# A hybrid encoder step on one core: the whole last prompt tile goes by fetched expert rows, the bias line is stored in eight pieces, and each v tile brings its own gelu tile

## What is computed

```python
q = (xb @ wq).reshape(nb, PEER_HEADS, 2, PEER_DKEY // 2)           # 8 heads, 2 x 64
s = jnp.einsum('nhpd,hpkd->nhpk', q, sub_keys)                     # 128 keys each
sv, si = lax.top_k(s, PEER_TOPK)                                   # 16 best of either half
cand = (sv[:, :, 0, :, None] + sv[:, :, 1, None, :])               # 256 sums
fv, fi = lax.top_k(cand, PEER_TOPK)                                # 16 experts per head
g = jax.nn.softmax(fv, axis=-1)
u, vv = expert_u[eidx], expert_v[eidx]                             # tables of 16384 x 1024
act = jax.nn.gelu(jnp.einsum('nhkd,nd->nhk', u, xb), approximate=False)
out = jnp.einsum('nhk,nhkd->nd', g * act, vv)
```

## Time and profile before

| | |
|---|---|
| median of 3 runs | 2180.13 us (2179.73 to 2186.38) |
| profiled execution, its own time | 2187.16 us |
| its span, first to last instruction | 2185.4 us |
| busy share of the span: PE, DVE, ACT, POOL | 92%, 59%, 42%, 36% |
| mean granted TensorE clock | 0.961 |
| moved by DMA | 421.70 MB |

### The profile page before, as it was taken

The page is one execution under the profiler, slowest core; times in us unless marked ns, Lnnn a source line. Parts: engine busy times, 40 slices in busy tenths (PEclk is TensorE's granted clock), DMA queues, the critical chain, the costliest instruction groups (busy, mean ns, idle before and its releaser), DMA issues. The chain is left out here.

```text
span 2185.4 us, 32122 instructions
## 1 busy us (share of the span) xinstructions
PE 2011.7 (92%) x11629; PEld 1826.0 (84%) x11629; DVE 1282.9 (59%) x2482; ACT 918.6 (42%) x2008; POOL 797.6 (36%) x780
## 2 busy tenths in 40 slices
PE   7299987998996999999999999996999999999997
PEld 6298876886895998898999999996989889998896
DVE  2014352334613299999999855552566666666666
ACT  4012112224314233585888888882333323323333
POOL 4142322322321201485898888880011111111110
PEclk9699988999997999999999999998999999999999
DMA  6431135222606166788889899988679879889873
GB/s 150 71 87 39 39 127 91 81 77 89 210 20 137 41 178 184 203 256 239 254 233 264 247 265 265 259 255 271 221 253 293 284 252 298 284 273 298 269 252 108
DMA packets 304465, 421.70 MB, mean 193 GB/s; under 512 B 32116, under 2 KB 248692, under 8 KB 300724
## 3 DMA queue, kind: packets, MB, share of 16 engines
q1 hardware_dynamic: 276660, 318.98, 50.4%
q0 software_dynamic: 27648, 100.68, 15.0%
HBM read 346.43 MB, written 72.42 MB: 192 GB/s over the span
## 5 line engine op out<-in xcount | busy, mean ns | idle before, releaser
L1311 PE MATMUL ps<-x_high,uT_high 128*128 128x448 f32 x1024 | 383.9, 375 | 15.8 <-DVE uT_low L1303 15.8
L1888 PE MATMUL ps<-hid_high,v_high 128*128 128x448 f32 x1024 | 376.9, 368 | 22.8 <-DVE hid_low L1861 22.8
L1555 POOL TENSOR_SCALAR area<-iota_row,chosen 128x128 f32<-128x128 f32 x448 | 376.5, 854 | 2.6
L1888 PE MATMUL ps<-hid_low,v_high 128*128 128x448 f32 x1024 | 375.7, 367 | 0.0
L1888 PE MATMUL ps<-hid_high,v_low 128*128 128x448 f32 x1024 | 375.7, 367 | 0.0
L1311 PE MATMUL ps<-x_high,uT_low 128*128 128x448 f32 x1024 | 375.3, 367 | 0.0
L1311 PE MATMUL ps<-x_low,uT_high 128*128 128x448 f32 x1024 | 374.9, 366 | 0.0
L1834 ACT CAST v_high<-area 128x1024 fp32r<-128x1024 f32 x128 | 134.2, 1048 | 448.2 <-PE ps L1888 369.7
L1229 POOL DMA_INDIRECT gathered_rows<-in_peer_v_dram,gathered_index x96 | 96.8, 1009 | 570.1 <-DVE gathered_acc L1261 481.5
L1859 DVE TENSOR_TENSOR v_low<-area,v_high 128x1024 fp32r<-128x1024 f32 x128 | 156.8, 1225 | 233.7 <-ACT v_high L1834 233.7
L1303 DVE TENSOR_TENSOR uT_low<-u_turned,uT_high 128x1024 fp32r<-128x1024 f32 x128 | 159.3, 1244 | 158.8 <-ACT uT_high L1298 158.8
(11 more groups left out here) (289 smaller groups left out, 3731.5 us busy)
## 6 DMA issues: line engine op xcount, KB each, us to landing
u_nat<-in_peer_u_dram SPq DMA_DIRECT2D x512, 128.0 KB, 4.7
area<-in_peer_v_dram SPq DMA_DIRECT2D x128, 512.0 KB, 5.3
hidden<-gelu_out SPq DMA_DIRECT2D x128, 224.0 KB, 3.3
routing<-dense SPq DMA_DIRECT2D x28, 1024.0 KB, 6.1
w_raw<-in_w_in_dram SPq DMA_DIRECT2D x44, 512.0 KB, 4.0
area<-hidden SPq DMA_DIRECT2D x8, 1792.0 KB, 8.6
gelu_in<-hidden SPq DMA_DIRECT2D x8, 1792.0 KB, 9.5
routing_in<-routing SPq DMA_DIRECT2D x8, 1792.0 KB, 16.7
```

The lines of the kernel that those rows point to most:

```text
L1311: ins = self.nc.tensor.matmul(self.k.ps[:, b, 0:N], w[:, b, kk, :], x[:, kk, 0:N], start=(kk == 0 and p == 0), stop=(kk == KD - 1 and p == 2))
L1555: ins = nc.gpsimd.tensor_scalar(first[:, b % AREAS, f, :], iota[:, :], chosen[:, 0, c:c + 1], None, ALU.is_equal)
L1888: ins = nc.tensor.matmul(ps[:, kk, 0:N], v[:, b, kk * P:(kk + 1) * P], h[:, b, :], start=(n == 0 and p == 0), stop=(n == P - 1 and p == 2))
```

## The change

Three edits.

1. `MORE` is now a list of (first frame, frames) of tile 3 that are fetched: [(0, 128)]. All 128 frames of tile 3 fetch their 128 picks each, so `HALVED` = 0, N = 384, the routing has 96 batches and 24 groups of 16 frames in place of 112 and 28, `ALL` = 160 and the matmuls are 128 x 384. The copies that repack picks and x for the two half-tiles of frames fall away but for one each of index and weight. `posf` and `picked` move into an area that is free then. `Plan` is unchanged but reads the new numbers: 160 dots stand in the 110 steps 15 to 124 where 96 stood, and the first batch of routing is at step 46, not 27.
2. `rel_line` is stored in `PIECES` = 8 parts of 384 KB, one behind each of the weight tiles 5 to 12.
3. In `experts` the gelu tile of step n comes right behind v tile n, alone (192 KB), into the slot that step n-8 has left, and the routing tiles of 8 steps come in 4 parts of 384 KB behind four v tiles. The adds are spread evenly over steps 7 to 120.

The core of the diff:

```diff
-FETCHED = P // 2
-SETS = P // FETCHED
-HALVED = P - FETCHED
+MORE = [(0, P)]
+HALVED = min(lo for lo, _ in MORE)
 N = 3 * P + HALVED
...
+PIECES = 8
 AHEAD_LOADS = 64 if HALVED else 48
-MORE = PH * TOPK // SETS
-ALL = PICKS + MORE
+SETS = [P // f for _, f in MORE]
+TAKEN = [PH * TOPK // n for n in SETS]
+FROM = [PICKS + sum(TAKEN[:j]) for j in range(len(MORE) + 1)]
+ALL = FROM[-1]
+COPIES = 2 * sum(SETS)
...
             for i in range(2, EARLY + 4):
                 load_tile(i)
-                if i == 5:
+                if 5 <= i < 5 + PIECES:
                     sp.wait_ge(line_done, 1)
-                    sp.dma_start(k.line_dram, bcast(line, 1, P)).then_inc(line_stored, 16)
+                    rows = slice((i - 5) * P // PIECES, (i - 4) * P // PIECES)
+                    sp.dma_start(k.line_dram[:, rows], bcast(line, 1, P // PIECES)).then_inc(line_stored, 16)
...
         if m % ALL >= PICKS:
-            pool.wait_ge(self.more_ready, 32 * SETS)
+            pool.wait_ge(self.more_ready, 16 * COPIES)
         after(pool, self.used, m - RING + 1)
...
         @block.sync
         def _(sp):
-            def load_oct(q):
+            def load_routing(q, i):
+                groups = slice(NGRP * i // PARTS, NGRP * (i + 1) // PARTS)
                 after(sp, hid_low_done, OCT * (q - 1))
-                sp.dma_start(gelu[q % 2], k.gelu_dram[q * OCT:(q + 1) * OCT].rearrange("a j n -> j a n")).then_inc(in_loaded[q % 2], 16)
-                sp.dma_start(routing[q % 2].rearrange("j g a n -> j g (a n)"),
-                             k.route_dram[:, :, q * OCT:(q + 1) * OCT, :].rearrange("g j a n -> j g (a n)")).then_inc(in_loaded[q % 2], 16)
-
-            load_oct(1)
+                sp.dma_start(routing[q % 2][:, groups].rearrange("j g a n -> j g (a n)"),
+                             k.route_dram[groups, :, q * OCT:(q + 1) * OCT, :].rearrange("g j a n -> j g (a n)")).then_inc(in_loaded[q % 2], 16)
+
             for n in range(V, P):
                 sp.wait_ge(v_low_done, n - V + 1)
                 sp.dma_start(v_nat[:, n % V, :], peer_v[0, n * P:(n + 1) * P, :]).then_inc(v_loaded[n % V], 16)
-                if n % OCT == 2 and n // OCT + 1 < P // OCT:
-                    load_oct(n // OCT + 1)
+                if n >= OCT:
+                    sp.wait_ge(hid_low_done, n - OCT + 1)
+                    sp.dma_start(gelu[:, n % OCT, :], k.gelu_dram[n]).then_inc(v_loaded[n % V], 16)
+                q, i = divmod(n + OCT - V, OCT)
+                if i < PARTS and q < P // OCT:
+                    load_routing(q, i)
...
-                if n >= 8 and n % 5 != 0 and (n - 8) * 4 // 5 < ALL:
+                while added[0] < min(ALL, (n - 6) * ALL / (P - 14)):
                     gathered.add(dve, added[0])
                     added[0] += 1
```

More of the change, by code:

```diff
@@ L1231, in fetch, with part @@
                                           ).then_inc(self.fetched[m % RING], 16)
+    @staticmethod
+    def part(m):
+        return sum(m >= f for f in FROM[:-1])
     def arrived(self, eng, m):
@@ L1367, in _ @@
                 sp.dma_start(gathered.x[g * TS:(g + 1) * TS, 0, :], gathered.x[0:TS, 0, :]).then_inc(gathered.x_ready, 16)
[L1368 to L1371, removed]
+            sp.wait_ge(row_scaled, 1 + len(MORE))
+            copies = EXTRA - 1
+            for j, (lo, frames) in enumerate(MORE):
+                for g in range(SETS[j]):
+                    if g * frames != lo:
+                        copies += 1
+                        sp.dma_start(gathered.x[g * frames:(g + 1) * frames, 1 + j, :], gathered.x[lo:lo + frames, 1 + j, :]).then_inc(gathered.x_ready, 16)
+            sp.wait_ge(gathered.x_ready, 16 * copies)
         @block.scalar
@@ L1515, in step @@
                     sp.wait_ge(pick_done, 1)
[L1516 to L1519, removed]
+                    for j, (lo, frames) in enumerate(MORE):
+                        rows, mine = slice(lo, lo + frames), slice(FROM[j], FROM[j + 1])
+                        for g in range(SETS[j]):
+                            to, picks = slice(g * frames, (g + 1) * frames), slice(g * TAKEN[j], (g + 1) * TAKEN[j])
+                            sp.dma_start(gathered.index[to, mine], flat[rows, picks]).then_inc(gathered.more_ready, 16)
+                            sp.dma_start(gathered.weight[to, mine], picked[rows, 2, picks]).then_inc(gathered.more_ready, 16)
                 for b in plan.routing.get(n - 3, []):
@@ L1797, in experts @@
     V = 4
+    PARTS = 4
     v_nat, v_loaded, in_loaded, gelu, routing = k.v_nat, k.v_loaded, k.in_loaded, k.gelu_in, k.routing_in
-    gelu = (gelu[0], hold("gelu_in1", [P, OCT, N])[:, :, :])
+    gelu = gelu[0]
     routing = (routing[0], hold("routing_in1", [P, NGRP, OCT, GRP])[:, :, :, :])
@@ L1920, in _ @@
                 if t == 3:
-                    for c in range(2):
-                        ins = nc.tensor.matmul(ps[HALVED:P, 2 * t + c, :], same[:, TS:], gathered.acc[:, 1, c * 512:(c + 1) * 512], start=True, stop=True)
+                    for j, (lo, frames) in enumerate(MORE):
+                        cols = slice(TS + lo - HALVED, TS + lo - HALVED + frames)
+                        for c in range(2):
+                            ins = nc.tensor.matmul(ps[lo:lo + frames, 2 * t + c, :], same[:, cols], gathered.acc[:, 1 + j, c * 512:(c + 1) * 512],
+                                                   start=True, stop=True)
                 ins.then_inc(turned, 1)
```

50 lines of the change are left out of this document (29 added, 21 removed).

## The result

| | before | after |
|---|---|---|
| median of 7 runs each, us | 2179.73 (2173.55 to 2186.38) | 2158.23 (2147.05 to 2169.22) |
| ratio after / before | | 0.9898, interval 0.9868 to 0.9929 |
| span of the profiled execution, us | 2185.4 | 2155.2 |
| mean granted TensorE clock | 0.961 | 0.947 |

The account below looks back on a forecast made before the run. PE was taken as busiest, with DVE, POOL and DMA just under it. Terms -30 - 3 + 40 + 22 - 67 = -38 us took the profiled 2187.2 to 2149, or 2142 us at the median; range 2085 to 2210.

Parts of the forecast that it names:

- What bounds the kernel: Whole kernel: PE has the largest share; the change moves its work to DVE, POOL and DMA, which stand just under it.
- Narrower matmuls: `search` and `experts`: 384 columns take 0.174 and 0.177 us a matmul, 175 us less PE work in all.
- `rel_line` in pieces: Projection: weight tiles no longer wait behind the whole store, so PE's stall shrinks; -30 us, bounds -41 and -15.
- Steps 0 to 14: Start of `search`, 749 to 830 us: a narrower matmul gives back at most DVE's time without a dot; -3 us.
- With the sort: `search`, 830 to 1232 us: DVE, 98% busy with 97 dots for 58, sets the length; +40 us, bounds +26 and +53.
- third rival: `search` from step 46: POOL is locked for all of DVE's two-input time; sum +52, 2232 us; chance 0.08.
- After the sort: `search`, 1232 to 1482 us: POOL, stretched by DVE's two-input work, needs 272 us; +22 us, bounds -28 and +74.
- The change-over: End of `search` to `experts`, 1482 to 1523 us: the same loads move, a seventh smaller; 0.
- `experts`: Last stage: even steps of 4.5 us at a DMA rate near the high end, 576 us; -67 us, bounds -99 and +14.
- PE stays the only bound: Rival, whole kernel: POOL and DVE absorb the dots and DMA keeps up; -134, 2046 us; chance 0.12.
- DMA bounds `experts`: Rival, `experts`: DMA stays at 322 GB/s, so the stage takes 657 us, +14 for -67; total 2223 us; chance 0.12.
- The pieces bring nothing: Rival, projection: each tile waits as long in all, the rest as forecast; -8, 2172 us; chance 0.06.

Follow-up runs that it names:

- e2: The changed kernel with only the second half of tile 3 fetched, as before (N = 448, 96 fetches): 2121.95 us, ratio 0.9709.
- e3: The changed kernel with four slots for fetched rows in place of three: 2128.89 us, ratio 0.9753.
- e5: The changed kernel with POOL making two of the four one-hots of each batch from the fifth batch on: 2110.88 us, ratio 0.9659.
- e6: The changed kernel with each dot only summing its fetched row, one input in place of two: 2108.58 us, ratio 0.9659.
- e1: The kernel before with the bias line stored in eight pieces and nothing else changed: 2137.21 us, ratio 0.9793.

## Why the prediction was right, and where not

- **What bounds the kernel.** Right: what leaves PE arrives at DVE, POOL and the DMA. Of the 175 us that PE gives free nothing is left: e2 against after, the first edit by itself is a loss of 36 us with three slots; e3, with four, is 7 us slower than e2.
- **Narrower matmuls.** The distances are 0.175 and 0.173 us for 0.174 and 0.177.
- **`rel_line` in pieces.** The mechanism was right, the size off: -46.5 for -30, beyond the bound of -41. The failed step is "Before it could not be through before 104.8 + 36 = 141". Tile 11 is the last of the run, as I had it, but its work was mis-sized. Between 104.8 and 159.2 us PE makes 432 matmuls, not 288: 96 for tiles 6 and 7, 240 for tiles 8 to 11 (60 a tile, not 48), and 96 for the gates, whose weights come from `wg_raw`. They take 54.4 us, where I had 36. With the change PE is through the same run at 117.1 us, with 0.2 us of waiting for a tile in all; tile 11 is split at 91 us, not 103. That is 42.1 us less, the whole stall of 41.04 and about 1 us of the slow start after it. The forecast waits of some 10 us did not come, since tiles came every 7.9 us. The other 4.4 us come from one place, PE's wait for `pT` at 345.6 us: 10.9 us before and 6.3 after. ACT, which makes `pT`, waits there for the transfer `gates<-mkT`, 16.2 and 11.5 us. I can name no edit for it; over the nine profiles with pieces this wait is 6.3 to 9.4 us, and `search` starts between 696.3 and 703.3 us.
- **Steps 0 to 14.** -5.1 for -3.
- **With the sort.** +44.6 for +40, but for two reasons where I gave one. In steps 15 to 45 DVE is the bound as forecast, 99% busy, and +16.6 us come from its dots (44 where 26 stood). In steps 46 to 81 it is not 98% busy but 93%: e5 and e6 take POOL's time and leave DVE nearly all of its own (223 and 222 us for 232), and the stage falls from 248.3 to 227.5 and 223.6 us. Only then is DVE 98 and 99% busy and the bound. So 21 to 25 of the +28.0 are POOL's, and 3 to 7 are DVE's, over the 220.3 us that PE took before. The step that failed is the claim that "DVE is 98% busy to the end of the sort" and alone sets the length. It is the third rival's mechanism in the place that it named, at less than its +38; that the sum still came out near is luck of sizes.
- **After the sort.** +25.4 for +22, by the mechanism given. POOL is busy 262 us and waits 12 more at its own issues, 273 in all for the 272 forecast. The one-hots' excess is 178.6 - 208 x 0.606 = 52.6 us; a fetch takes 1.353 us where I had 1.10, and so the lock hits it too. e6 and the overlaps in the trace of after show the cause. The Trainium skill (SBUF — State Buffer, "SBUF: two separate sides") names it: DVE with two SBUF inputs and a GpSimd instruction that reads SBUF exclude each other. The trace agrees (one-hots have a mean of 1120 ns beside a two-input instruction of DVE, 598 beside a transpose). My reading that "the fetches' descriptors are no part of it" was wrong: fetches beside a two-input instruction have a mean of 1589 ns, the others at most 1031.
- **The change-over.** -1.7 for 0.
- **`experts`.** -45.8 for -67. Steps are 4.67 us on average for 4.5, and not even but 4.16 with stalls. The step that failed is "so I go near the high end: 4.5 us a step": the price was taken from the DMA's rate, and the ring only from its mean, 3.3 us a step at 5.8 us of landing. The landing rose to 7.6 us (median), the fetch on POOL from 0.94 to 1.62 us, and the dense work of a step stands between two adds; so 73 of 158 adds found their row not there. e3, with four slots, gives 572 us, the 576 of the forecast. "Near 365 GB/s" was too high: 351 over 500 us, 327 over the stage. The Trainium skill's limit (DMA: Bandwidth & Descriptors, "Specifications") had led to an estimate of 591 us, near the 597 measured, but it is not what holds the stage: e3 moves the same tiles in 572, and slices of 12.5 us carry up to 380 GB/s. That it came near is luck as well.
- **The rivals.** "PE stays the only bound" fell: from step 15 on it is the bound in no stage. "DMA bounds `experts`" fell as the only bound: 327 GB/s with 93% busy was in part the result of waits, since e3 carries 340. Its price was wrong too: 657 us takes 1.654 MB for all 128 steps, 212 MB, but rows are fetched for some 114 of them and the stage moves 195 MB, 606 us at 322 GB/s. That is near the 597 measured, so the total alone could not have ruled it out; e3 does, with the same bytes in 572 us. "The pieces bring nothing" fell with e1.
- **What was missed.** The granted clock. Where PE waits for POOL or DVE it falls to the lower of its two levels (1.2 GHz) and comes back: 0.93 to 0.95 over steps 15 to 123, 1.00 before. After the sort it is the lower one in 27 of 276 us, in seven stretches, six of which follow a wait of PE of 1.9 to 2.9 us. The longer distances add up to 9.6 us after the sort and to as much in `experts` (3.5 and 1.0 before); some 6 and 5 us of them lie at the lower clock.

## What to carry to other kernels

Work taken off the busiest engine pays only until the next one is full, and of the three sizes tried (64, 96 and 128 fetched frames of the tile) the middle one was the best: sum every engine in every stage, with the stretched durations and not the medians, before choosing the size. A ring must be sized for the landing under the new load plus the longest work between two uses, since 160 rows in place of 96 and a landing of 7.6 us in place of 5.8 turned a ring that never waited into 92 us of waits. Before pricing a removed stall, count the instructions that stand behind it; here 432 matmuls were taken for 288, and the smallest edit was worth more than the whole change.

## What the runs showed of the hardware

- The instruction that issues a fetch on POOL is stretched by DVE's two-input work as one-hots are: after the sort its mean is 1589 ns beside a two-input instruction and at most 1031 in any other place, and in steps 15 to 45 a mean of 1348 ns falls to 967 when the dots have one input (e6). In `experts` its median is 936 ns when adds are 94 and 1619 ns when they are 158, with the same transfer.
- A store of 8 partitions to DRAM and a load of 128 partitions, one behind the other on a queue, overlap: 118 GB/s in 63 to 105 us, where the store alone moves about 52.
- In slices of 12.5 us one core moved up to 380 GB/s, with a mean of 351 over 500 us.
